# A float32 transformer stack on one core: extra TensorE products ahead of two norms

## The reference, cut to what matters

```python
def second_block(x, ...):
    f1 = _swiglu(_rmsnorm(h, ffn1_pre_g), ffn1_w_gate, ffn1_w_up, ffn1_w_down)
    h = h + 0.5 * _rmsnorm(f1, ffn1_post_g)
    u = _rmsnorm(h, mix_pre_g)                 # border to the mixer
    proj = u @ w_in
    ...
    mixed = (sigmoid(g_a) * y_a + sigmoid(g_b) * y_b) @ w_out
    h = h + _rmsnorm(mixed, mix_post_g)
    f2 = _swiglu(_rmsnorm(h, ffn2_pre_g), ...) # border to the second macaron part
    return h + 0.5 * _rmsnorm(f2, ffn2_post_g)
```

## Time and profile before

| what | value |
|---|---|
| median of 3 runs | 3533.44 us (3533.19 to 3537.11) |
| profiled execution, in all | 3537.51 us |
| its span | 3535.7 us |
| mean granted TensorE clock | 0.98 |
| PE busy | 3414.5 us (97%), 18490 records |
| DVE, ACT busy | 57%, 44% |

### The profile page before, as it was taken

The page is one execution under the profiler, slowest core; times in us unless marked ns, Lnnn a source line. Parts: engine busy times, 40 slices in busy tenths (PEclk is TensorE's granted clock), DMA queues, the critical chain, the costliest instruction groups (busy, mean ns, idle before and its releaser), DMA issues.

```text
span 3535.7 us, 45270 instructions
## 1 busy us (share of the span) xinstructions
PE 3414.5 (97%) x18490; PEld 2867.6 (81%) x18490; DVE 2012.3 (57%) x2032; ACT 1538.6 (44%) x1565; POOL 321.5 (9%) x364
## 2 busy tenths in 40 slices
PE   7999889999999999999999999999999999999998
PEld 4875678888888888888888899998888788888886
DVE  2655567775566554444444578995455544444445
ACT  3323346653455443333334455663443443333333
POOL 1000000000000000000000157661000000000000
PEclk9999999999999999999999999999899999999999
DMA  9998667776666665566556656677235555555553
GB/s 337 359 335 345 182 198 226 222 224 222 190 187 190 193 198 190 190 190 195 189 190 192 181 144 168 181 194 239 86 106 183 171 189 189 189 196 193 188 189 138
DMA packets 529863, 713.21 MB, mean 202 GB/s; under 512 B 12951, under 2 KB 347103, under 8 KB 524192
## 3 DMA queue, kind: packets, MB, share of 16 engines
q1 hardware_dynamic: 509888, 647.01, 57.9%
q0 software_dynamic: 15024, 59.53, 5.0%
q10 hardware_dynamic: 4784, 4.27, 0.4%
HBM read 702.09 MB, written 11.82 MB: 202 GB/s over the span
## 4 chain that ended last, share of the span: by engine, by line
PE 81%; DVE 8%; ACT 4%; issue 3%; DMA 2%; POOL 1%; ACTq 0%; SPq 0%; DVEq 0%; POOLq 0%
PE ps L2769 9%; PE ps L2771 9%; PE ps L2770 9%; PE ps L2636 8%; PE ps L2637 8%; PE ps L2640 8%; PE ps L2568 7%; PE ps L2569 3%; DVE w_lo L1517 3%; ACT w_hi L920 2%; PE ps L2587 2%; DMA stage<-in_w_ada 2%; PE ps L2588 1%; PE ps L2589 1%; PE ps L2600 1%
## 5 line engine op out<-in xcount | busy, mean ns | idle before, releaser
L1517 DVE TENSOR_TENSOR w_lo<-stage,w_hi 128x2048 fp32r<-128x2048 f32 x480 | 1108.3, 2309 | 1105.6 <-ACT w_hi L920 1093.9
L920 ACT ACTIVATE w_hi<-stage 128x2048 fp32r<-128x2048 f32 x476 | 911.3, 1915 | 1306.7 <-PE ps L2771 561.7
L2769 PE MATMUL ps<-w_hi,xt 128*128 128x512 f32 x1408 | 551.4, 392 | 3.4 <-DVE xt L1579 1.8
L2771 PE MATMUL ps<-w_hi,xt 128*128 128x512 f32 x1408 | 549.1, 390 | 0.0
L2770 PE MATMUL ps<-w_lo,xt 128*128 128x512 f32 x1408 | 548.8, 390 | 0.0
L2568 PE MATMUL ps<-xt,w_hi 128*128 128x512 f32 x1320 | 471.6, 399 | 6.8 <-DVE w_lo L1517 6.8
L2636 PE MATMUL ps<-w_hi,hid_hi 128*128 128x512 f32 x1152 | 449.6, 390 | 5.8 <-DVE w_lo L1517 5.8
L2637 PE MATMUL ps<-w_lo,hid_hi 128*128 128x512 f32 x1152 | 448.3, 389 | 0.0
L2569 PE MATMUL ps<-xt,w_lo 128*128 128x256 f32 x1320 | 371.3, 281 | 0.0
L2640 PE MATMUL ps<-w_hi,hid_lo 128*128 128x512 f32 x1152 | 354.8, 389 | 0.0
L2769 PEld LDWEIGHTS ps<-w_hi,xt 128*128 128x128 f32 x1408 | 265.0, 188 | 58.7 <-issue 2.3
(11 more groups left out here) (444 smaller groups left out, 4567.1 us busy)
## 6 DMA issues: line engine op xcount, KB each, us to landing
stage<-in_w_in SPq DMA_DIRECT2D x88, 1024.0 KB, 5.7
stage<-in_w_up SPq DMA_DIRECT2D x88, 1024.0 KB, 5.8
stage<-in_ffn_w_gate SPq DMA_DIRECT2D x88, 1024.0 KB, 5.1
stage<-in_ffn_w_up SPq DMA_DIRECT2D x88, 1024.0 KB, 5.1
stage<-in_ffn_w_down SPq DMA_DIRECT2D x88, 1024.0 KB, 5.5
stage<-in_w_ada SPq DMA_DIRECT2D x64, 1024.0 KB, 7.8
stage<-in_w_down SPq DMA_DIRECT2D x44, 1024.0 KB, 5.7
stage<-in_w_out SPq DMA_DIRECT2D x32, 1024.0 KB, 5.5
```

The source lines that it names most:

```text
L920: act.activation(w_hi[:, u % 2 * UNIT:(u % 2 + 1) * UNIT], slot(u % SLOTS), ACT.Copy).then_inc(hi_made, 1)
L1517: dve.tensor_tensor(w_lo[:, part], slot(u % SLOTS), w_hi[:, part].bitcast(F32), ALU.subtract).then_inc(split_made, 1)
L2769: pe.matmul(dst, chunk(xt_hi, k, m), wh, start=k == 0, stop=False)
L2771: last = pe.matmul(dst, chunk(xt_lo, k, m), wh, start=False, stop=k == KC - 1)
```

## The change

A function `keep_busy(b, count)` issues `count` products of 128 x 128 by 128 x 512 of `hid_hi` with itself into bank b; nothing reads the result. It is called in five ways: after every second of the 30 small products in `bias_rows` (14 times one product), after `bias_rows` behind a wait for the first four pieces of x_nat (8) and behind a wait for all eight (10), and after out2 behind a wait for its first half to be taken (14) and behind one for the mean square (6). No other engine's program differs.

```diff
--- before.py
+++ after.py
@@ -2707,6 +2707,11 @@
             for u in range(2):
                 part(name, u, dsts[u], range(8, KC), norm_index, True)
 
+        def keep_busy(b, count):
+
+            for _ in range(count):
+                pe.matmul(bank(b), hid_hi[:, 0:P], hid_hi[:, 0:512], start=True, stop=True)
+
         def bias_rows():
 
             pe.wait_ge(S["oh_in"], 64)
@@ -2717,6 +2722,8 @@
                     a = 255 + P * m - 16 * i - 31
                     last = pe.matmul(bank(7, m * 240 + i * 16, 16), oh_fwd[:, a:a + P], relb[:, :],
                                      start=True, stop=True)
+                    if i % 2:
+                        keep_busy(5, 1)
             last.then_inc(S["biasc_made"], 1)
 
         def ffn(n):
@@ -3046,6 +3053,10 @@
 
         ffn_rows(1, norm_ffn1)
         bias_rows()
+        pe.wait_ge(S["piece_made"], NEW_AT[4] + 4)
+        keep_busy(5, 8)
+        pe.wait_ge(S["piece_made"], NEW_AT[4] + 8)
+        keep_busy(5, 10)
         norm(3)
         def bring(pr):
 
@@ -3316,6 +3327,10 @@
             for tile in range(2):
                 pair_tile(plan["wo"][1] + w, tile, bank(4 + w % 4, tile * T, T), po_hi, po_lo, w % 2)
         rows_phase("out2", 8, hid_hi, hid_lo, ready=S["mixed_made"], last=True)
+        pe.wait_ge(S["rows_taken"], 2 * rows_index["out2"] + 1)
+        keep_busy(0, 14)
+        pe.wait_ge(S["norm_var"], ROOT_AT[6] + 1)
+        keep_busy(0, 6)
         norm(4, range(2))
 
         def norm_ffn2(u):
```

## The result

| | before | changed |
|---|---|---|
| median of 14 runs | 3535.55 us | 3544.17 us |
| lowest and highest | 3529.77 to 3541.03 | 3540.81 to 3547.82 |
| profiled execution, span | 3535.7 us | 3544.0 us |
| mean granted clock | 0.980 | 0.981 |

The account below looks back on a forecast made before the run. TensorE, busy 97% of the span, was taken as the bound. Mixer border +4.4 and second border -1.6 gave +2.8 us: 3540.3 on the profiled execution, 3536 on the median, range 3528.5 to 3541.

Parts of the forecast that it names:

- 14 x 0.23: Mixer border, clock held: the 14 products among bias_rows' small ones cost 0.23 us each, 3.2 us together.
- 6 to 7 products x 0.43: Mixer border, clock lost at 1988: the added products left in bias_rows cost 0.43 us each, 2.7 us together.
- small products with an occasional dense one: Stretch 2492.0 to 2499.8, taken as nearest to the new bias_rows: held the clock 8 us, then lost it.
- Lost: Forecast case: clock falls in bias_rows, taken at 1988; +4.4 us at the mixer border, 3536 on the median; chance 0.54.
- clock held in bias_rows: Rival: dense products keep the clock high at the mixer border, -2.0 us there, -1.6 at the second, 3529.8; chance 0.28.
- The early fall: Mixer border, clock falling at 1984.5 as before: bias_rows end at 1998.7, norm(3) at 2012.6, +6.6 us.
- Low to the end: Rival: clock falls at 1984.5, the 18 products run low throughout, second border gives nothing; +7.8 us, 3541.2; chance 0.07.
- The base: Whole kernel: starting time for the median forecast, 3533.44 us, the median of the runs shown.
- The 18 products: Behind bias_rows, clock lost: 12 run low and 6 high, so norm(3) starts at 2003.0 and ends at 2010.4.
- The added waits: Four waits on PE's queue at both borders: none of their semaphores depends on the products, and norm(3), norm(4) wait later anyway.
- The second border: Before the second macaron block: first product 0.4 us sooner, 7 low products in place of 13, -1.6 us.
- The range: Whole kernel: 3528.5 to 3541 us, taking in both signs and the wandering of the median.

Follow-up runs that it names:

- e2_interleave_alone: Changed kernel with only the 14 products among the small ones, the other 38 taken out: median 3542.94 us, ratio to before 1.0022.
- e8_small_128_rows: Changed kernel with the 30 small products widened to 128 rows (no bias) and the second border's 20 products left out: ratio to before 1.0012.
- e7_same_rows: Changed kernel with the 14 products among the small ones cut to 33 rows and the second border's 20 left out: ratio to before 1.0016.
- e1_no_interleave: Changed kernel without the 14 products among the small ones, the 18 and 20 others kept: median 3534.73 us, ratio to before 0.9996.
- e4_four_kinds: Changed kernel with four row-count and format combinations in the 14 places, second border's 20 left out: one trace, down11's last product to values' first 36.36 us.

## Why the prediction was wrong

- *The step that failed is the price of a product among the small ones.* "14 x 0.23" and "6 to 7 products x 0.43" took prices from rows in which a product follows its like. In bias_rows a product cost 0.53 at the high level (5 times) and 0.83 at the low one (9 times), as each change of row count holds back the next weight load. bias_rows took 21.0 us, not 14.0: 5.1 us are the stalls themselves, and the rest is mostly work that was still to be done when the clock fell. The 7.0 us more than explain the whole miss at this border, +10.84 against +4.4.
- *The warning was in the trace of before,* in the very stretch that the forecast took for its nearest row. From 2494.70 on products of 15 rows (L3234) and of 128 rows (L3226) take turns there, and at each change the load starts only with its product. The width of the weights changes there too (15 and 128 columns), so these rows show that such a change costs something, not which part of it (first PE's row, then PEld's):

```profile
2496.27 1.10 PE L3234 MATMUL ps<-vc_n,cmp_t 15*128 15x64 f32 x8
```

```profile
2495.73 0.33 PEld L3226 LDWEIGHTS ps<-ident,cmp_s 128*15 128x15 f32 x4
2496.27 0.96 PEld L3234 LDWEIGHTS ps<-vc_n,cmp_t 15*128 15x128 f32 x8 [0.21 <-issue]
```

- *The same stretch was misread for the clock.* It isn't "small products with an occasional dense one": 256-column products fill it until 2494.5, and then come short products alone, under which the clock fell at 2499.9, 5.4 us after the last dense one started. It said nothing of how a mixture fares.
- *"Lost", and where.* Lost was right. The clock fell at 1987.7 and 1988 was taken, but that was luck. The forecast expected the added products to put off the fall. It came 4.9 us after the first small product in this trace, but 2.0 to 2.8 us after it in the other five traces with products in bias_rows (2.7 in e2_interleave_alone, whose code there is the same), and 1.7 to 2.7 in the six without. So that they put it off isn't shown. With the price right the clock was lost just the same (e8_small_128_rows). The rival "clock held in bias_rows", at 0.28, never came up in the six traces with products in bias_rows.
- *The early fall was summed too low.* For a fall at 1984.5 the forecast has bias_rows end at 1998.7. By its own prices 12 records and 3 products are done by then, and 48 x 0.213 + 11 x 0.43 = 15.0 us are left: 1999.5, and +7.4 in place of +6.6 at the border. e7_same_rows, with that price and such a fall, measured +7.4. "Low to the end" moves by as much, to about 3542. The measured time is above that too.
- *The base.* The forecast counted from 3533.44, the median of three runs; the median of 14 is 3535.55. Of the 8.2 us between 3536 and 3544.17 that is 2.1.
- *The 18 products.* 6.3 us, 6.5 predicted; norm(3) 7.06, 7.4 predicted. Both within 0.4 us.
- *The added waits.* The forecast had them cost nothing, and that was right: PE has no idle time before the 18 products, and 0.21 us before the last six of the 20. But with bias_rows at 21 us the 18 products filled nothing, as diag had been ready for 7.1 us before the first of them.
- *The second border.* -1.8 us, -1.6 predicted, by the steps given: first product 0.46 us sooner (0.4), 7 low products (7), the fall close to the end of the idle time. By the page's statement on transposes (the Trainium skill, "TensorE: Matmul & The Clock Gate", section "Part 4: PE-mode transpose"), that they don't count as PE activity like other products, the fall was sure there. It fell in all three traces that have the 20 products and the idle time behind norm(4), in two of them within that idle time and in e1_no_interleave 0.1 us behind it. No run here had the transposes without that idle time and without other products, so whether they count isn't settled.
- *"Low to the end"* gave 3541.2 by other steps (a fall at 1984.5, no return in the 18 products). Neither took place, so its nearness to the result is no credit.
- *The range* was made of the cases' ends, each with the same two prices, 0.23 and 0.43. The price of a product between unlike ones stood in no row that was read, and it was put at that of a product between like ones, with nothing above it in any case. So the sum at the first border could only come out too low.

## What to carry to other kernels

A filler product is free only in time in which TensorE would wait. Elsewhere it is work, and among products of another row count dear work: among products of 33 rows, one of 128 cost 0.53 us at the high clock and 0.83 at the low one, about twice what it costs between its like. Count the wait first (2.7 us of it here, and 32 products), then put as many products there as it holds, and close the idle time on the far side of the short work too. When two kinds of instruction are to be mixed, look in the trace for a place at which such kinds already meet, and lay the starts of the weight loads beside those of the products.

## What was not expected of the hardware

- The stall at a change of row count: at both changes the weight load starts together with its product. It is about 0.15 us each at the high level and 0.2 at the low one (groups of 0.98 and 1.68 us against 0.68 and 1.28 in e7_same_rows). A change of the number format alone shows none (L2730 in e4_four_kinds).
- A 512-column product after every second small one didn't hold the clock, neither in groups of 0.98 us (changed kernel) nor of 0.68 us (e8_small_128_rows): it went to 0.50 within 2.0 to 4.9 us of the first small product in all of them.
- In the changed kernel PE kept the high level through 4.3 us in which it had only 8 short records (2792.4 to 2796.7), and the return came after 2.8 us of dense work, where it took 5.8 us before.
- One kernel's runs spread over 11 us (before: 3529.77 to 3541.03), and its time between two fixed points of the program over 5.7 us from trace to trace, and the intervals of the medians reach 3 us to either side. Smaller differences can be read only within a border of a trace, and there too two traces of the same code gave a D1 2 us apart.
